# Steady products in the mixers of a hybrid decoder step, and a buffer of their own for the meta tokens' queries

## What is computed

```python
def stick_breaking(q, k, v, q_pos, k_pos, bias):
    z = (jnp.einsum('bqhd,bkhd->bhqk', q, k).astype(jnp.float32) * (DH_A ** -0.5)
         + bias.astype(jnp.float32)[None, :, None, None])
    mask = k_pos[None, :] < q_pos[:, None]
    log_beta = jax.nn.log_sigmoid(z)
    log_keep = jnp.where(mask, jax.nn.log_sigmoid(-z), 0.0)
    later = lax.cumsum(log_keep, axis=3, reverse=True) - log_keep
    att = jnp.where(mask, jnp.exp(log_beta + later), 0.0)
    return jnp.einsum('bhqk,bkhd->bqhd', att.astype(v.dtype), v)

# rwkv_branch, per head and token
    def step(state, inp):
        r_t, w_t, k_t, v_t, kk_t, a_t = inp
        sa = jnp.einsum('bhvk,bhk->bhv', state, kk_t)
        state = (state * w_t[:, :, None, :]
                 - sa[..., None] * (kk_t * a_t)[:, :, None, :]
                 + v_t[..., None] * k_t[:, :, None, :])
        return state, jnp.einsum('bhvk,bhk->bhv', state, r_t)
# then a norm per head, a bonus and a gate
```

## Time and profile before

| | |
|---|---|
| median of 3 runs | 3437.68 us |
| lowest and highest | 3432.95 and 3444.43 us |
| the profiled execution | 3451.49 us |
| its span, first to last instruction | 3449.8 us |
| TensorE's mean granted clock | 0.958 |
| TensorE, VectorE, ScalarE, GpSimd busy | 95%, 58%, 39%, 19% |
| HBM traffic over the span | 88 GB/s |

### The profile page before, as it was taken

One profiled execution on the slowest core, in us unless ns is written; L12 is line 12 of the kernel. 1 busy time (PEld: TensorE's weight loads), 2 busy tenths in 40 slices (PEclk: granted clock), 3 DMA queues, 4 the chain that ended last, 5 costly groups with the idle time before them and its releaser, 6 DMA issues. The chain is left out here.

```text
span 3449.8 us, 56008 instructions
## 1 busy us (share of the span) xinstructions
PE 3274.4 (95%) x20556; PEld 2956.9 (86%) x20556; DVE 2007.6 (58%) x3776; ACT 1342.5 (39%) x2645; POOL 664.3 (19%) x1026
## 2 busy tenths in 40 slices
PE   8999988989899999999999999999889999999998
PEld 7999756656566799999999989998579999999997
DVE  6444436566657686555555566533668655555555
ACT  5444334555555663222322244213456322232223
POOL 0000122333333051111111021001215111111102
PEclk9999986889889999999999999999989999999999
DMA  5333472323222351111111312233434211111131
GB/s 151 129 128 128 149 240 84 100 55 103 53 58 50 98 173 62 53 45 43 44 53 43 125 27 70 84 123 120 168 102 144 72 49 43 48 43 54 43 124 52
DMA packets 371571, 304.76 MB, mean 88 GB/s; under 512 B 74413, under 2 KB 333873, under 8 KB 371396
## 3 DMA queue, kind: packets, MB, share of 16 engines
q1 hardware_dynamic: 356168, 249.95, 24.1%
q0 software_dynamic: 14080, 50.45, 4.1%
q10 hardware_dynamic: 1152, 2.11, 0.2%
HBM read 223.09 MB, written 79.37 MB: 88 GB/s over the span
## 5 line engine op out<-in xcount | busy, mean ns | idle before, releaser
L1515 PE MATMUL ffn_ps<-parts_hi,ffn_w_lo 128*128 128x368 f32 (+2 forms) x1152 | 379.2, 329 | 0.0
L1513 PE MATMUL ffn_ps<-parts_hi,ffn_w_hi 128*128 128x368 f32 (+2 forms) x1152 | 378.9, 329 | 0.0
L481 PE MATMUL ffn_ps<-ffn_h_hi,ffn_w_hi 128*128 128x368 f32 (+2 forms) x1008 | 336.1, 333 | 9.0 <-DVE ffn_h_lo L1150 5.4
L483 PE MATMUL ffn_ps<-ffn_h_hi,ffn_w_lo 128*128 128x368 f32 (+2 forms) x1008 | 332.9, 330 | 0.0
L482 PE MATMUL ffn_ps<-ffn_h_lo,ffn_w_hi 128*128 128x368 f32 (+2 forms) x1008 | 332.2, 330 | 0.0
L1514 PE MATMUL ffn_ps<-parts_lo,ffn_w_hi 128*128 128x368 f32 (+2 forms) x1008 | 331.1, 328 | 0.0
L1268 DVE TENSOR_TENSOR mix<-ffn_ps,mix 128x368 f32<-128x368 f32 (+2 forms) x432 | 229.7, 538 | 148.0 <-PE ffn_ps L483 148.0
L872 ACT ACTIVATE ffn_w_hi<-ffn_sums 128x512 fp32r<-128x512 f32 x144 | 84.7, 624 | 472.4 <-PE ffn_ps L483 359.7
L481 PE MATMUL ffn_ps<-parts_hi,ffn_w_hi 128*128 128x368 f32 (+2 forms) x768 | 257.9, 336 | 2.9 <-DVE ffn_w_lo L1078 2.9
L482 PE MATMUL ffn_ps<-parts_lo,ffn_w_hi 128*128 128x368 f32 (+2 forms) x768 | 253.7, 330 | 0.0
L483 PE MATMUL ffn_ps<-parts_hi,ffn_w_lo 128*128 128x368 f32 (+2 forms) x768 | 252.8, 329 | 0.0
(11 more groups left out here) (592 smaller groups left out, 8128.3 us busy)
## 6 DMA issues: line engine op xcount, KB each, us to landing
out_w_first<-in_w_ffn_gate_dram SPq DMA_DIRECT2D x44, 512.0 KB, 3.8
ffn_w_raw<-in_w_ffn_up_dram SPq DMA_DIRECT2D x44, 512.0 KB, 3.9
first_w_raw<-in_w_in_ab_dram SPq DMA_DIRECT2D x27, 512.0 KB, 4.0
out_w_first<-in_w_ffn_down_dram SPq DMA_DIRECT2D x22, 512.0 KB, 3.5
ffn_w_raw<-in_w_ffn_down_dram SPq DMA_DIRECT2D x22, 512.0 KB, 3.4
rwkv_prep<-xT POOLq DMA_DIRECT2D x4, 2208.0 KB, 7.5
qkv_proj<-head_out_sb POOLq DMA_DIRECT2D x16, 552.0 KB, 3.6
atts_v_page<-in_cache_v_dram POOLq DMA_DIRECT2D x32, 256.0 KB, 6.1
```

Source lines behind the costliest of these rows:

```text
L481: pe.matmul(out, w_hi, x_hi, start=first, stop=False)
L483: return pe.matmul(out, w_lo, x_hi, start=False, stop=last)
L1513: pe.matmul(out, w[0], x_hi, start=first and k == 0, stop=False, skip_group_check=True)
L1515: mm = pe.matmul(out, w[1], x_hi, start=False, stop=k == HALF - 1, skip_group_check=True)
```

## The change

Two parts, both in `attention_and_rwkv`.

**Steady products.** A helper `steady(n)` in TensorE's program puts n steady products into attention's scores bank `Z`. If scores have been made, it first waits until the last of them are out of the bank (`z_scaled`). It is called behind strict 1, before and behind tokens 0, behind each of the seven `first` items (TensorE has no instruction of its own for them), before the tokens of groups 0 and 1 of each later pair, before level 4's `p` of group 2 of each pair, behind `y` and `s` of each sample tile, before the second `st_in` of pairs 1 to 3, and before the three means of the last pair.

**Queries.** The meta tokens' queries get a buffer `q_meta` and a semaphore `meta_loaded`. `q_in` now serves the 16 long blocks alone: block b's queries are loaded at the start of long block b - 1. Those of the meta tokens are loaded at the start of a pair's second long block, right behind the queries of the third.

```diff
--- before.py
+++ after.py
@@ -2758,6 +2758,9 @@
     rests = [sum(not st[6] for st in steps[:n + 1]) for n in range(NS)]
     block_at = [sum(st[6] for st in steps[:n]) for n in range(NS)]
     block_starts = [n for n in range(NS) if first[n]]
+    LONG = len(q_blocks)
+    long_starts = [n for n in block_starts if steps[n][2] == G]
+    long_at = [sum(n <= t for n in long_starts) - 1 for t in range(NS)]
     HALF = N_META + 2 * G
     HIGH_DONE = sum(top + 1 for q0, top in q_blocks if q0 >= HALF)
     LOW_TOP = q_blocks[2][1]
@@ -2878,6 +2881,7 @@
         post_ps, B_POST = ps[:, 1, :], 1
 
         q_in, k_in = s.sb("q", [P, 2, 2, 2, G], F32R), s.sb("k", [P, 2, TP], F32R)
+        q_meta = s.sb("q_meta", [P, 2, 2, N_META], F32R)
         v_in = s.sb("v", [P, 9, 2, DH])
         bias8 = s.sb("bias8", [P, NH])
         zs, keep = s.sb("zs", [P, 3, 2, G]), s.sb("keep", [P, 3, 2, G])
@@ -2888,6 +2892,7 @@
         att = s.ctx.enter_context(nc.psum_tensor("attp_ps", [P, 3, 2, G], F32))
         Z, LOG, O = 0, 1, 2
         in_bank = slice(0, CW)
+        meta_loaded = s.sem("meta_loaded")
         bias_in, q_loaded, k_loaded, v_loaded = s.sem("bias_in"), s.sems("q_loaded", 2), s.sems("k_loaded", 2), s.sems("v_loaded", 2)
         z_mm, z_scaled, z_capped, exp_done, log_done = (s.sem(n) for n in
                                                         ("z_mm", "z_scaled", "z_capped", "exp_done", "log_done"))
@@ -2941,13 +2946,22 @@
                 sp.dma_start(v_flat[:, 1:LOW_TOP + 1, :], v_tokens[N_META:HALF, to].rearrange("(j p) n -> p j n", p=P)
                              ).then_inc(v_loaded[1], 16)
 
+            def query(i, x, q0, width):
+                at = ((2 + x) * NPAIR + i) * P
+                return qk_parts[at:at + P, q0:q0 + width].rearrange("(h d) t -> d h t", d=DH)
+
             def load_q(b):
-                i, q0, width = steps[block_starts[b]][0:3]
+                i, q0, width = steps[long_starts[b]][0:3]
                 for x in range(2):
-                    at = ((2 + x) * NPAIR + i) * P
-                    of = qk_parts[at:at + P, q0:q0 + width].rearrange("(h d) t -> d h t", d=DH)
                     for half in range(2):
-                        sp.dma_start(q_in[pair(half), b % 2, x, :, 0:width].bitcast(F32), of).then_inc(q_loaded[b % 2], 16)
+                        sp.dma_start(q_in[pair(half), b % 2, x, :, :].bitcast(F32), query(i, x, q0, width)
+                                     ).then_inc(q_loaded[b % 2], 16)
+
+            def load_meta(i):
+                for x in range(2):
+                    for half in range(2):
+                        sp.dma_start(q_meta[pair(half), x, :, :].bitcast(F32), query(i, x, 0, N_META)
+                                     ).then_inc(meta_loaded, 16)
 
             def load_gate(i):
                 sp.dma_start(gate[:, :].unsqueeze(1), early.of_pair(i, 5, 1)).then_inc(gate_loaded, 16)
@@ -3056,10 +3070,13 @@
                         sp.wait_ge(z_mm, t)
                         part_waits(sp, parted)
                         load_k(sp, i, 1)
-                    if part == 0 and 0 < t < NS and first[t] and block_at[t] + 1 < len(block_starts):
+                    if part == 0 and 0 < t < NS and t in long_starts:
                         sp.wait_ge(z_mm, t)
                         part_waits(sp, parted)
-                        load_q(block_at[t] + 1)
+                        if long_at[t] + 1 < len(long_starts):
+                            load_q(long_at[t] + 1)
+                        if long_at[t] % LONG == 1:
+                            load_meta(i)
                     i, n = (t - 4) // PAIR_STEPS, (t - 4) % PAIR_STEPS
                     if part == 2 and n == HIGH_DONE and 0 <= i and i + 1 < NPAIR:
                         sp.wait_ge(pv_mm, t - 4)
@@ -3136,6 +3153,14 @@
             def bk(N):
                 return be_ka[:, pair_of(N) % 2, :, :]
 
+            scored = []
+
+            def steady(n):
+                if scored:
+                    pe.wait_ge(z_scaled, 2 * len(scored))
+                    part_waits(pe, parted)
+                idle_products(pe, c, att[:, Z, :, :].rearrange("p x n -> p (x n)"), n)
+
             def post_bank(users):
                 for counter, name in users:
                     pe.wait_ge(act_done if counter is ACTS else dve_done, counter(name))
@@ -3316,6 +3341,10 @@
                     kind = item[0]
                     if kind == "strict":
                         strict(item[1])
+                        if item[1] == 1:
+                            steady(4)
+                    elif kind == "first":
+                        steady(2)
                     elif kind == "gather":
                         g = item[1]
                         post_bank(last_use)
@@ -3323,11 +3352,17 @@
                         last_use = [(DVE, f"m{g}.1")]
                     elif kind == "tokens":
                         g = item[1]
+                        if g % NG < 2 and g != 1:
+                            steady(4 if g == 0 else 3 if g % NG == 0 else 1)
                         post_bank(last_use)
                         tokens(g)
+                        if g == 0:
+                            steady(6)
                         last_use = [(ACTS, f"tok{groups[g][-1]}")]
                     elif kind == "p":
                         _, g, l = item
+                        if l == LEVELS[0] and g % NG == 2:
+                            steady(4)
                         post_bank(last_use)
                         half_products(g, l)
                         last_use = [(DVE, f"p{g}.{l}.{halves(g) - 1}")]
@@ -3343,10 +3378,16 @@
                             sa_step(N, g, slot, k, L)
                         elif kind == "y":
                             y_step(N, slot, k, L, cn)
+                            if is_sample(N):
+                                steady(3)
                         else:
                             s_step(N, slot, k, L)
+                            if is_sample(N):
+                                steady(2)
                     elif kind == "st_in":
                         _, i, k = item
+                        if i and k:
+                            steady(2)
                         post_bank(last_use)
                         pe.wait_ge(state_in, 32 * (i + 1))
                         for b in range(4):
@@ -3371,6 +3412,8 @@
                         last_use = [(DVE, f"states_out{i}.{k}.1")]
                     elif kind in ("mean", "var"):
                         _, i, ch = item
+                        if i == NPAIR - 1:
+                            steady(2)
                         post_bank(last_use)
                         pe.wait_ge(act_done, ACTS(f"y{NT * i + LAST}" if kind == "mean" else f"sq{i}"))
                         part_waits(pe, parted)
@@ -3386,9 +3429,13 @@
                     part_waits(pe, parted)
                 i, q0, width, kt, lo, diag, last = steps[n]
                 keys, lo, width, k0 = shape(n)
-                b = block_at[n]
+                b = long_at[n]
+                of_block = q_in[:, b % 2, :, :, :] if width == G else q_meta[:, :, :, :]
                 if first[n]:
-                    pe.wait_ge(q_loaded[b % 2], (b // 2 + 1) * 64)
+                    if width == G:
+                        pe.wait_ge(q_loaded[b % 2], (b // 2 + 1) * 64)
+                    else:
+                        pe.wait_ge(meta_loaded, 64 * (i + 1))
                     part_waits(pe, parted)
                 if n % PAIR_STEPS == 0:
                     pe.wait_ge(k_loaded[0], (i + 1) * 32)
@@ -3403,12 +3450,13 @@
                 for hh in range(2):
                     for x in range(2):
                         mm = pe.matmul(att[0:keys, Z, hh, lo:width], k_in[:, hh, k0:k0 + keys],
-                                       q_in[:, b % 2, x, hh, lo:width], start=x == 0, stop=x == 1 and not diag,
+                                       of_block[:, x, hh, lo:width], start=x == 0, stop=x == 1 and not diag,
                                        skip_group_check=True)
                     if diag:
                         mm = pe.matmul(att[0:keys, Z, hh, lo:lo + keys], unit[0:keys, 0:keys],
                                        not_earlier[0:keys, 0:keys], start=False, stop=True, skip_group_check=True)
                 mm.then_inc(z_mm, 1)
+                scored.append(n)
 
             def sums(n):
                 keys, lo, width, k0 = shape(n)
```

## The result

| | runs | median us | lowest to highest |
|---|---|---|---|
| before, same session | 4 | 3435.31 | 3428.98 to 3444.43 |
| after | 4 | 3460.41 | 3459.40 to 3462.64 |

The changed kernel takes 1.0072 times as long (95% interval 1.0047 to 1.0096): 25 us slower. The forecast was 3427.8 us with a range of 3402 to 3452. Its sign is wrong, and its range doesn't hold the time. A second set of five runs gave 3458.72 us, a ratio of 1.0055 (1.0036 to 1.0074). The profiled execution took 3462.64 us around a span of 3460.9, against 3451.49 around 3449.8 before.

The account below looks back on a forecast made before the run. The prediction took TensorE, 95% busy, to be the bound after the opening, at a clock its own short waits lower. Terms +10.8, +33.1, -7.0, -44.8 and -2.0 sum to -9.9 us: 3427.8 us from the 3437.7 median, range 3402 to 3452.

Parts of the forecast that it names:

- The opening, +10.8: Start of the mixers' stage: 28 products delay scores, clamps and the first inverse, +10.8 us (bounds +5 and +24).
- The other 60 products, +33.1: Products at y, s, st_in, p, tokens and last means: their time less the waits they fill, +33.1 us exposed.
- less four waits: Behind the sample tiles' y: 12 products, 10.3 us, less four waits of 0.56 to 0.71 (2.4), leaving 7.9 us.
- Slack, -7.0: Idle TensorE time ahead of the stage's tail: a quarter of 27.9 us absorbs delays, -7.0 us (bounds 0 and 14).
- The clock, -44.8: Half-clock stretches at or soon after the sites, 119.4 us, go, at 0.22 to 0.56 per low microsecond: -44.8 us.
- about 24 us in every pair: Sign in the changed profile: the stretch from (p, 2, 4) to tile 3 takes about 24 us in every head pair.
- all terms are absolute, so I carry them to the median: Whole sum: -9.9 us, made on the profiled 3451.5 us execution, applied unscaled to the 3437.7 us median.
- Queries, -2.0: Scores 50: the separate meta-token query buffer removes a 1.97 us wait for loads, -2.0 us; eight issues in a row priced 0.
- B: Rival: clock falls move instead of going, half the clock's gain comes back, +12.5, 3450.2 us; chance 0.25.
- D: Rival: the products don't hold the clock, +34.9, 3472.6 us; chance 0.06.
- C: Rival: low time costs 0.56 everywhere, the clock gives 66.9, sum -32, 3405.7 us; chance 0.17.
- The three signs that were to show the prediction wrong: Stage low time staying above 80 us, the opening costing 5 or 20, or slack taking back most of the exposed time.

Follow-up runs that it names:

- e4: The unchanged kernel executed again for a second profile: 3430.3 us.
- e7: The changed kernel run again, all 94 products: 3458.7 us, ratio 1.0055.
- e15: The changed kernel a third time, one execution: 3461.1 us.
- e8: The unchanged kernel executed again for a third profile: 3430.3 us.
- e16: The unchanged kernel executed again for a fourth profile: 3431.3 us.
- e3: The changed kernel with every steady product removed, so only the queries' buffer remains: 3441.2 us, ratio 0.9999 to the kernel before.
- e9: The kernel before plus nine steady products, three before the tokens of groups 5, 10 and 15, without the queries' buffer: 3441.0 us, ratio 1.0001.
- e11: The kernel before plus three steady products in the opening, behind the sixth step of the first inverse: 3438.6 us, ratio 1.0001.
- e5: The changed kernel keeping only the queries' buffer and the 12 products before tokens of groups 5, 6, 10, 11, 15, 16: 3435.8 us, ratio 0.9987.
- e14: e9 plus eight steady products behind the sample tiles' s: 3447.0 us, ratio 1.0019 to the kernel before.
- e10: The changed kernel keeping only the queries' buffer and the 20 products behind the sample tiles' y and s: 3451.3 us, ratio 1.0040.
- e2: The changed kernel keeping only the opening's 28 products and the queries' buffer: 3451.7 us, ratio 1.0025 to the kernel before.
- e13: e1 without the twelve products behind the sample tiles' y: 3451.0 us, ratio 1.0037 to the kernel before.
- e6: The changed kernel without the products of the opening and before tokens; 54 products and the queries' buffer stay: 3458.4 us, ratio 1.0049.
- e1: The changed kernel without the opening's 28 steady products: 3452.1 us, ratio 1.0032 to the kernel before.

## Why the prediction was wrong

**The opening, +10.8: right.** TensorE's timeline after:

```profile
499.01 5.39 PE L471 MATMUL attp_ps<-constants 128*128 128x512 f32 x8
...
509.24 5.32 PE L471 MATMUL attp_ps<-constants 128*128 128x512 f32 x12
513.99 0.74 PE L3452 MATMUL attp_ps<-mixers_q,mixers_k 128*128 128x128 f32 x2
...
515.98 3.67 PE L471 MATMUL attp_ps<-constants 128*128 128x512 f32 x8 [0.81 <-ACT mixers_zs L3595]
...
521.31 5.39 PE L471 MATMUL attp_ps<-constants 128*128 128x512 f32 x12 [1.02 <-ACT mixers_zs L3595]
...
528.19 1.96 PE L471 MATMUL attp_ps<-constants 128*128 128x512 f32 x4 [1.02 <-ACT mixers_zs L3595]
```

Scores 0 start at 513.99 (513.5 was predicted), and each batch waits for ScalarE's eviction as foreseen. VectorE's queue answers the earlier trace rows:

```profile
515.87 0.29 DVE L3807 TENSOR_SCALAR mixers_keep<-mixers_zs 128x256 f32<-128x256 f32 x1 [10.04 <-ACT mixers_zs L3595]
516.11 0.07 DVE L2653 MEMSET mixers_blocks<- 64x16 f32 x1
...
521.20 0.43 DVE L3807 TENSOR_SCALAR mixers_keep<-mixers_zs 128x512 f32<-128x512 f32 x1 [3.27 <-ACT mixers_zs L3595]
...
528.08 0.43 DVE L3807 TENSOR_SCALAR mixers_keep<-mixers_zs 128x512 f32<-128x512 f32 x1 [3.14 <-ACT mixers_zs L3595]
...
531.58 0.37 DVE L2664 COPY mixers_turned<-mixers_blocks 64x256 f32<-64x256 f32 x1
```

The three clamps end at 516.2, 521.6 and 528.5, and the inverse's last copy at 532.0 (530.6 was predicted). Tile 9's x is 11.4 us later than in the first profile and 12.3 later than in e4. In the changed kernel's other two profiles, e7 and e15, it is 10.5 later than in e4, so the term lies between 10.5 and 12.3 us.

**The other 60 products, +33.1: the mechanism right, y too small.** Compared with e4 the shifts at the four p are 0.3, 3.2, 4.8 and 1.6, 10.0 in all (10.2 predicted). At tokens 5, 10 and 15 they are 1.48, 1.66 and 1.75, together 4.9 (4.7), and from just ahead of the last pair's first mean to its last variance 5.2 (5.2 was predicted for the means alone; the six products that weren't counted are in it). The four sites behind y cost 3.7, 3.5, 3.5 and 2.0, 12.7 in place of 7.9. The failed step there is "less four waits", at full clock: with the last of the sixteen small products the clock had already fallen. s, st_in and the tokens of 6, 11 and 16, 5.1 us together in the sum, are taken as predicted here.

**Slack, -7.0: nothing.** The prediction had no row for it, only "I take a quarter" of the idle time left. Between two sites, wherever both kernels are at the same clock, after takes what e4 takes: from tile 10's x to gather 7 10.46 and 10.45 us, from tile 23's x to tile 25's 24.68 and 24.67. A shift, once made, stays. The likely reason, argued and not tried: most of these waits end with VectorE's or ScalarE's work on TensorE's own earlier products, which is then late by as much.

**The clock, -44.8: right for that execution, not for the median.** Behind the p sites, in windows of after that answer the first three of the earlier trace rows:

```profile
592.31:615.16 22.85, 21.53 (x225) 15.98 (x225) 17.43 (x42) 14.08 (x31) 12.11 (x29) 1.00 0.12 28
748.66:774.07 25.41, 22.56 (x229) 16.11 (x228) 17.90 (x42) 13.43 (x30) 10.84 (x30) 1.00 0.12 26
914.15:937.37 23.22, 21.16 (x224) 15.53 (x223) 16.55 (x41) 12.27 (x28) 8.13 (x26) 1.00 0.11 26
```

The first gained 10.9 us (33.77 before; 11.1 was predicted for it and its like), and "about 24 us in every pair" holds. From tile 7 to gather 6 the gains are 8.4, 6.8 and 5.7, 20.9 in all. The prediction had more for these windows: 21.0, another 3.7 for the stretch from 836.0, which lies in the second of them, and the 2.0 of the queries, whose wait stands there too. Without that wait 18.9 us came back for the 47.3 low us that the three windows held, 0.40 each and not 0.56.

Against the first profile the stage's balance closes at the predicted gain too: 11.4 for the opening and 38 for the sites (33.1 and the 4.8 that y cost more), less 44.8 by the clock and 2 at scores 50, make +2.6, and the stage is 2.45 us longer. In part that is luck: 153 low us went, not 119.4. 24 of them stood in the opening, where no gain was seen, and the other 129 gave about 45 us, 0.35 each in place of 0.375.

But the prediction then carried this term, "absolute", to a median 13.8 us below the profile. Part of those 13.8 us was low time too: the profiled execution has 289 us of it and the median of the 94 runs 268, and 21 us at 0.32 to 0.42 are 7 to 9 us. What isn't low in the typical execution can't be won back. By the medians 109 low us went (268 to 159). Less some 22 in the opening, and at 0.35 each, they give about 30 us in place of 44.8, an estimate from these figures.

Against e4's stage the same balance is 12.3 + 38 less 26, +24 (675.5 - 651.4 = 24.1): the 26 is what the balance leaves for the clock, for the 102 low us that went, 20 of them in the opening, where they cost nothing. **This is the largest single step that failed**, "all terms are absolute, so I carry them to the median". A term that consists of bad luck in the profiled execution has to be scaled to the typical one. It isn't the only one: slack, measured at nothing, and y, 12.7 in place of 7.9, are 11.8 us together, and in the profiled executions, where the base plays no part, the sign was wrong as well (-9.9 forecast, +11.1 came).

The rule of the Trainium skill, page "TensorE: Matmul & The Clock Gate", section "HAM oscillation — how this bites in real kernels", counts half of the throttled time as lost. These runs give 0.32 over whole executions and 0.42 over the stage: the rule's half is too much for a stage that VectorE and ScalarE share.

**Queries, -2.0: the waits went, the time didn't change.** The 1.97 us wait at scores 50 is not in every execution. It is 3.22 us in e8. In e16 it is 0.37, with 2.73 at scores 75. In e4 the same scores start without one:

```profile
816.82 0.67 PE L3405 MATMUL attp_ps<-mixers_q,mixers_k 128*128 128x128 f32 x2
```

In none of the profiles of a kernel with the buffer do scores 50 or 75 wait for queries. The eight issues in a row, priced at 0 under the cover of p's products, do cost once that cover is gone, as the prediction said they would. SP's queue and the p behind it in e3:

```profile
721.62 2.89 SPq L2957 DMA_DIRECT2D mixers_q<-qk_parts  x4
724.55 2.56 SPq L2963 DMA_DIRECT2D mixers_q_meta<-qk_parts  x4
727.23 0.51 SPq L3014 DMA_DIRECT2D rwkv_t<-mixers_blocks  x1
```

```profile
733.67 0.63 PE L3234 MATMUL rwkv_ps<-mixers_tu,mixers_nn 64*64 64x64 f32 x11 [3.10 <-issue]
```

and in e4:

```profile
721.21 2.54 SPq L2950 DMA_DIRECT2D mixers_q<-qk_parts  x4
724.36 0.34 SPq L3000 DMA_DIRECT2D rwkv_t<-mixers_blocks  x1
```

```profile
730.99 0.68 PE L3209 MATMUL rwkv_ps<-mixers_tu,mixers_nn 64*64 64x64 f32 x16 [1.41 <-issue]
```

The inverse's transfer is issued 2.9 us later, 0.4 of which the queue was late already, and the wait before p grows by 1.7 us; a second pair shows 1.3. So the buffer has a price at p. Overall e3 is at 0.9999, with an interval of 8 us to either side, in which -2.0 would fit as well.

**How the 32.6 us between forecast and median add up.** The profiled executions first: -9.9 was forecast, 3462.64 - 3451.49 = +11.1 came. Of these 21.0 us slack is 7.0, y 4.8 and the opening 0.6; 0.9 stand ahead of the stage and 7.7 behind it, where the diff touches nothing: 21.0. Those last 8.6 are the clock's scatter in the main. Behind the stage the first profile after has 87 us of low time and the first before 64, and 23 us more at 0.32 are 7.4. Over all 18 profiles the time behind the stage goes with its low time at 0.27 us for each (correlation 0.81), and the unchanged kernel alone spans 64 to 85 us there. The other 11.6 us are the base: the median that the forecast was carried to is 13.8 under before's profile, after's median only 2.2 under its own.

**Rivals.** B was nearest: slower, because the clock gives less than 34.9 us. Its deciding point was right, its price (+12.5) too small. Its mechanism, falls that move, is seen at one site of e9. It isn't the cause here: in the changed kernel the falls are gone, but fewer of them were there to remove than the profile said. D is refuted, since the products hold the clock, and so is C's 0.56 for all of the low time (0.32 to 0.42). The three signs that were to show the prediction wrong all stayed silent: the stage's low time is 48.5 us, not above 80; the opening costs 10.5 to 12.3, not 5 or 20; slack took back nothing. They tested the terms and not the base. The stretch from s to p is 38.3 us in the second pair against 36.7 in the first profile and 36.3 in e4, as far as it was allowed to go.

**A sum over all kernels.** With 0.32 us for each low microsecond taken off, every kernel's median gives its time at equal clock. The kernel before stands at 3440.0 - 0.32 x 268 = 3354. Above it stand: e3 0 us, e9 and e11 4, e5 6, e14 16, e10 18, e2 20, e13 and e6 33, e1 39, after 55. The products' time, at 0.86 us each, is 0, 8 and 3, 10, 15, 17, 24, 46 and 46, 57, 81. So half of it is paid at the tokens' sites, two thirds to all of it nearly everywhere else. (This is an estimate: the medians come from several sessions, and e2's low time was worth less than the line says.) The changed kernel removes 109 low us (268 - 159), worth 35, for 55. That this makes the 20 us between the medians is no check, since the 55 come from the same two medians. Against the prediction's terms it says that the products cost 55 and not 34.9 (its sum without the clock), and that the clock gave 35 and not 44.8: by this sum the larger miss is in the costs.

**What stays open.** The two sums weigh the misses differently, and no run separates the base from slack and y. Whether products in a bank of their own, which wait for nobody, would be cheaper wasn't tried.

## What to carry to other kernels

Before a price is put on a lowered clock, know how much of it the typical execution has: compare the profiled execution's time and mean clock with those of other runs, and scale the term to the median, not the sum's end alone. A product that only keeps TensorE busy was paid for here with half to all of its time, unless the whole batch fits between the moment its bank is free and the end of the wait; at 0.86 us for one and 0.32 us for each low microsecond, it has to remove 2.7 us of low time, and here the 94 removed 1.2 each. A gain that a window shows behind a site counts only if the low time of the whole stage goes down with it, and an experiment that keeps one part of a change has to keep what makes that part work: e9 left out the queries' buffer and ran into the wait that it removes.

## What the runs showed of the hardware

- The same program on the same data spends between 0.955 and 0.966 of full clock in 94 executions, and takes 3426 to 3453 us with it. Two profiles of it differ by 51 us of low time in the stage alone (201.4 and 150.2).
- TensorE's clock fell in a stretch in which TensorE counts as busy without a gap, at the end of sixteen products of 8 columns, 0.88 us of idle time 4 to 5 us ahead of it, and stayed low for 3.4 us of steady products.
- Low time is not worth the same everywhere: 0.40 us for each low microsecond from tile 7 to gather 6, 0.32 over whole executions, 0.27 behind the stage, and no gain to be seen in the opening, where 24 us of it went.
- A low stretch of 6.8 us began at each of the two waits for DMA (2.98 and 2.64 us) that e9 has at scores 50 and 75. e5 has neither the waits nor the stretches.
- Four DMA issues on SP's queue took 2.5 to 2.9 us, and a transfer behind four more of them was issued 2.5 us later.
